# Seven stage boundaries of a two-block transformer kernel: token parts, affine and split in PSUM, half norms on ScalarE

## What is computed

```python
# first block, i = 0, 1 (mix is the sconv/SSD mixer, then the forgetting attention)
x = layer_norm(ALPHA * x + mix, ln_mix_g[i], ln_mix_b[i])
x = layer_norm(ALPHA * x + conv_ffn(x, ...), ln_ffn_g[i], ln_ffn_b[i])
# second block, i = 0, 1 (y is grouped-query attention, then the chunked gMLP)
h = modulate(rmsnorm(x, norm1_g[i]), sh1, sc1)
...
x = x + g1[:, None, :] * y
h = modulate(rmsnorm(x, norm2_g[i]), sh2, sc2)
x = x + g2[:, None, :] * sq_relu_mlp(h, mlp_w_in[i], mlp_w_out[i])
```

## Time and profile before

| | us |
|---|---|
| median of three runs (2811.03 to 2811.69) | 2811.19 |
| the profiled execution | 2811.43 |
| its span in the trace | 2809.5 |
| PE busy | 2783.7 |
| DVE / POOL / ACT busy | 1303.3 / 1140.6 / 1081.2 |

### The profile page before, as it was taken

The page is one execution under the profiler, slowest core; times in us unless marked ns, Lnnn a source line. Parts: engine busy times, 40 slices in busy tenths (PEclk is TensorE's granted clock), DMA queues, the critical chain, the costliest instruction groups (busy, mean ns, idle before and its releaser), DMA issues.

```text
span 2809.5 us, 37915 instructions
## 1 busy us (share of the span) xinstructions
PE 2783.7 (99%) x13890; PEld 2287.7 (81%) x13890; DVE 1303.3 (46%) x1516; ACT 1081.2 (38%) x1574; POOL 1140.6 (41%) x472
## 2 busy tenths in 40 slices
PE   9999999999999999999989999999999999999999
PEld 8788888888878788888877788888888888888887
DVE  4157568863441658874276651123423642411232
ACT  3443443343332544333345643334333223432332
POOL 4333434444434024444435035444344434444443
PEclk9999999999999999999999999999999999999999
DMA  5322238742333027753321023332243322233332
GB/s 160 90 69 74 90 103 267 239 140 88 99 88 95 9 76 232 244 169 102 97 73 45 2 74 106 97 105 98 86 135 94 90 78 103 90 92 96 104 98 75
DMA packets 319812, 299.95 MB, mean 107 GB/s; under 512 B 16268, under 2 KB 251224, under 8 KB 319576
## 3 DMA queue, kind: packets, MB, share of 16 engines
q1 hardware_dynamic: 304680, 236.70, 28.2%
q10 hardware_dynamic: 15024, 61.75, 6.3%
HBM read 296.30 MB, written 2.11 MB: 106 GB/s over the span
## 4 chain that ended last, share of the span: by engine, by line
PE 46%; issue 36%; POOL 16%; DVE 1%; ACT 0%; POOLq 0%; DVEq 0%; ACTq 0%
POOL wlo L558 16%; PE ps L2034 8%; PE ps L2035 8%; PE ps L2036 8%; PE ps L1892 6%; PE ps L1894 6%; PE ps L1893 6%; PE ps L2319 1%; PE ps L2255 1%; PE ps L2284 1%; PE ps L2394 1%; PE ps L2065 0%; PE ps L2067 0%; PE ps L2066 0%; PE ps L1897 0%
## 5 line engine op out<-in xcount | busy, mean ns | idle before, releaser
L558 POOL TENSOR_TENSOR wlo<-raw,whi 128x1024 fp32r<-128x1024 f32 x444 | 1115.3, 2515 | 1630.6 <-ACT whi L616 1630.3
L1892 PE MATMUL ps<-xhi,whi 128*128 128x512 f32 x1824 | 718.0, 394 | 0.3
L1894 PE MATMUL ps<-xhi,wlo 128*128 128x512 f32 x1824 | 710.3, 389 | 0.0
L1893 PE MATMUL ps<-xlo,whi 128*128 128x512 f32 x1824 | 709.9, 389 | 0.0
L616 ACT ACTIVATE whi<-raw 128x1024 fp32r<-128x1024 f32 x444 | 466.3, 1052 | 288.9 <-PE ps L2036 167.8
L2034 PE MATMUL ps<-whi,ahi 128*128 128x512 f32 x1184 | 461.4, 390 | 0.7 <-DVE alo L1396 0.7
L2036 PE MATMUL ps<-whi,alo 128*128 128x512 f32 x1184 | 460.7, 389 | 0.0
L2035 PE MATMUL ps<-wlo,ahi 128*128 128x512 f32 x1184 | 460.6, 389 | 0.0
L1892 PEld LDWEIGHTS ps<-xhi,whi 128*128 128x128 f32 x1824 | 342.5, 188 | 73.1 <-issue 3.2
L1894 PEld LDWEIGHTS ps<-xhi,wlo 128*128 128x128 f32 x1824 | 342.3, 188 | 71.7
L1893 PEld LDWEIGHTS ps<-xlo,whi 128*128 128x128 f32 x1824 | 342.6, 188 | 71.0 <-issue 1.4
(11 more groups left out here) (282 smaller groups left out, 2858.0 us busy)
## 6 DMA issues: line engine op xcount, KB each, us to landing
adaraw<-in_ada_w ACTq DMA_DIRECT2D x64, 768.0 KB, 6.1
raw<-in_ffn_w_up SPq DMA_DIRECT2D x88, 512.0 KB, 4.0
raw<-in_mlp_w_in SPq DMA_DIRECT2D x64, 512.0 KB, 4.0
raw<-in_mlp_w_out SPq DMA_DIRECT2D x64, 512.0 KB, 3.7
raw<-in_gmlp_w_in SPq DMA_DIRECT2D x48, 512.0 KB, 3.8
raw<-in_sc_ssm_w_in SPq DMA_DIRECT2D x44, 512.0 KB, 3.8
raw<-in_ffn_w_down SPq DMA_DIRECT2D x44, 512.0 KB, 3.6
raw<-in_fox_w_in SPq DMA_DIRECT2D x24, 512.0 KB, 3.8
```

The costliest lines, as they stand in the source:

```text
L558: pool.tensor_tensor(wlo[:, j], raw[:, j], whi[:, j].bitcast(F32), ALU.subtract).then_inc(w_lo, 1)
L1892: pe.matmul(out, lh, rh, start=start, stop=False)
L1893: pe.matmul(out, lh, rl, start=False, stop=False)
L1894: return pe.matmul(out, ll, rh, start=False, stop=stop)
```

## The change

- `pe_busy` is no longer called at a boundary, and `xf` and `junk` are gone. The affine writes back to PSUM in place, and DVE splits out of PSUM.
- Blocks 0 to 3 go in token parts: at the six ordinary boundaries two parts of 256 tokens, at boundary 4 parts of 256, 128 and 128. Blocks 4 to 7 stay 512 wide.
- Part 1's eight transposes (tiles 0 and 1) stand inside the last tile of the tail, part 2's eight inside unit 2's products for part 1. `pe_f` runs blocks 0 to 3 of units 0 to 2 in 72 products of 128x256 and blocks 4 to 7 in 36 of 128x512. qkv and gv take the token tiles of a part.
- ScalarE does six of the eight half norms, at 1 to 3 with scale rstd and bias minus mean by rstd, for which DVE has a new small instruction a tile (`neg_mean`).
- At 1 and 3 the residual's four scales stand in and behind DVE's splits of blocks 6 and 7, and its four shifts go into the first FFN iteration, two behind each `hid_ff`. At 2 all eight stand beside the fqk stage's own splits.
- At 4 the last four units of dn1 ("deep") run tile by tile, with their activations held in the upper half of the split buffers, 24 products to a tile.
- The DMAs of `wf_raw` and `wsraw` are issued behind all affines of their boundary. In `pe_gm` tiles 0 and 1 of units 0 and 1 go first, and the transposes of `wsraw` wait for all eight blocks.

```diff
+    def act_xt_part(act, q, scale, bias, h, cols=PART):
+        c = cols[h]
+        for k in range(4):
+            act.wait_ge(xt_tp, XT0[q] + 4 * h + k + 1)
+            act.activation(ps[:, k, c], ps[:, k, c], ACT.Identity, scale=scale(k), bias=bias(k)).then_inc(xt_ev, 1)
...
+    def dve_xt_part(dve, q, h, cols=PART, ks=range(4)):
+        c = cols[h]
+        for k in ks:
+            dve.wait_ge(xt_ev, EV0[q] + 4 * h + k + 1)
+            dve.tensor_copy(xhi[:, k, c], ps[:, k, c]).then_inc(xt_hi, 1)
+            dve.wait_ge(xt_hi, XT0[q] + 4 * h + k + 1)
+            dve.tensor_tensor(xlo[:, k, c], ps[:, k, c], xhi[:, k, c].bitcast(F32), ALU.subtract).then_inc(xt_lo, 1)
...
+        dve_ln_moments(dve, r, name, 0)
+        dve_ln_moments(dve, r, name, 1)
+        for t in range(2):
+            dve_ln_inverse(dve, r, t)
+            norm(t, 0)
+        dve_ln_moments(dve, r, name, 2)
...
+        dve_xt_part(dve, r + 1, 0, ks=(2,))
+        dve_ln_moments(dve, r, name, 3)
+        dve_xt_part(dve, r + 1, 0, ks=(3,))
...
+        scale(0)
+        dve_xt(dve, r + 1, ks=(6,))
+        scale(1)
+        dve_xt(dve, r + 1, ks=(7,))
+        scale(2)
+        scale(3)
...
+                    if lo == 0:
+                        shift = resid_steps(dve, 2 * L)[1]
+                        shift(2 * b)
+                        shift(2 * b + 1)
...
+            for h in range(2):
+                for k in range(4):
+                    pe.wait_ge(xt_lo, XT0[q] + 4 * h + k + 1)
+                    for e in range(2):
...
+                        product(e, k, PART[h])
+                if h:
+                    for k in range(4, KD):
+                        pe_xt_late(pe, q, k)
+                for k in range(4):
...
+                    if not h and k == 2:
+                        pe_xt_part(pe, q, 1)
+                    product(2, k, PART[h])
+            for k in range(4, KD):
+                pe.wait_ge(xt_lo, XT0[q] + 4 + k + 1)
...
+    def pe_t_deep(pe, name, q):
+        H, S, A = PAIRS[name], U0[name], A0[name]
+        for t in range(NT):
+            for m in range(2 * H - 4, 2 * H):
...
+                if t == NT - 1:
+                    ins.then_inc(unit_done, 1)
+                    if m == 2 * H - 3:
+                        pe_xt_part(pe, q, 0)
...
+        for i, tiles in enumerate(DOUBLE_TILES):
+            last = i == 2
+            pe.wait_ge(res_add, 24 + (6, 7, 8)[i])
+            units(0, [0], blocks=XT0[4] + 4 * i, tiles=tiles, done=last)
+            if last:
+                for k in range(4, KD):
+                    pe_xt_late(pe, 4, k)
+            units(0, [1], blocks=XT0[4] + 4 * i + 2, tiles=tiles, done=last,
+                  mid=None if last else lambda: pe_xt_part(pe, 4, i + 1))
...
             if j == 1:
-                pe.wait_ge(xt_ev, 48)
+                pe.wait_ge(xt_lo, XT0[7])
                 pe.wait_ge(ws_in, 16)
```

More of the change, by code:

```diff
@@ L82 @@
 GU_SLOTS = 4
-NRM_ORDER = ((0, 0), (1, 0), (0, 1), (2, 0), (3, 0), (1, 1), (2, 1), (3, 1))
-KEEP_BUSY = (0, 18, 0, 16)
+PARTED = (1, 2, 3, 5, 6, 7)
+XT0 = [0]
+for _q in range(8):
+    XT0.append(XT0[-1] + (12 if _q in PARTED else 16 if _q == 4 else 8))
+EV0 = [_n - 8 for _n in XT0]
+PART = (slice(0, 256), slice(256, 512))
+DOUBLE_TILES = ((0, 1), (2,), (3,))
+DOUBLE_PART = (slice(0, 256), slice(256, 384), slice(384, 512))
+DEEP = "dn1"
 KEEP_START = (14, 24)
-NRM_COUNT = {t: NRM_ORDER.index((t, 0)) + 1 for t in range(4)}
 SMALL_AFTER, FORGET_AFTER, CUM_AFTER = 3, 8, 11
@@ L618, in build_in, with a_parts @@
     AHEAD = 3
+    def a_parts(name, m):
+        first = 2 * PAIRS[name] - 3
+        if name == DEEP and first <= m < first + 2:
+            return ahi2[:, m - first], alo2[:, m - first]
+        return ahi[:, m % 2], alo[:, m % 2]
     def bank_f(j):
@@ L1407, in dve_jit @@
         after_h0()
-        run(dve, H - 2, lambda e, j: step(H + 2, 2, e, j))
+        if name != DEEP:
+            run(dve, H - 2, lambda e, j: step(H + 2, 2, e, j))
+        else:
+            run(dve, H - 5, lambda e, j: step(H + 2, 2, e, j))
+            for m in range(2 * H - 3, 2 * H):
+                hi, lo = a_parts(name, m)
+                dve.wait_ge(a_hi, A + m + 1)
+                dve.tensor_tensor(lo, src[:, 2 * (m - H):2 * (m - H) + 2], hi.bitcast(F32), ALU.subtract).then_inc(a_lo, 1)
     def wait_tile(eng, r, name, t):
@@ L1674, in dve_qkv @@
         dve.wait_ge(qkg_in, 48)
-        dve.wait_ge(xt_lo, 40)
+        dve.wait_ge(xt_lo, XT0[5])
         for z in range(2):
@@ L1963, in unit @@
             ins.then_inc(unit_done, 1)
-        for s, v in first:
-            pe.wait_ge(s, v)
         if q == 0:
@@ L2019, in pe_f, with pe_t_unit @@
                     unit(i * RING + j, j)
-    def pe_t_unit(pe, start, e, j, bank0, lh, ll, first, blocks=None):
+    def pe_t_unit(pe, start, e, j, bank0, lh, ll, first, blocks=None, tiles=range(NT), done=True, mid=None):
         slot = (start + j) % RING
@@ L2027, in pe_t_unit @@
         for k in range(2):
+            if mid and k:
+                mid()
             if blocks is not None:
                 pe.wait_ge(xt_lo, blocks + k + 1)
-            for t in range(NT):
+            for t in tiles:
                 out = ps[:, bank0 + t]
```

370 lines of the change are left out of this document (222 added, 148 removed).

## The result

The changed kernel takes 2796.43 us in the median of five runs (2794.49 to 2797.13), the kernel before 2811.19 (2810.92 to 2811.69, five runs too); the ratio is 0.9946, with a 95% interval of 0.9935 to 0.9956. The profiled execution took 2796.46, against 2811.43 before, so 14.97 us went. The forecast was 2791, with 2785 to 2803 as its range: it was faster as forecast, by three quarters of the 20 us that the sum promised. The narrower range of 2787 to 2795, which was given the chance of 0.58, was missed by 1.4 us.

The account below looks back on a forecast made before the run. PE's stream bounds the kernel, except in 54.15 us of gaps at seven boundaries, set by the latency of the DVE, PE, ACT, DVE chain. The terms summed to -20.3 from 2811.43, giving 2791 us, range 2785 to 2803.

Parts of the forecast that it names:

- The gap and the half products: Boundaries 1 and 3: the 5.87 us gap goes; 72 half products at 0.12 us replace 36 full ones, +0.45 us.
- rival A: Half products take 0.165 to 0.188 us each: +2 us at five boundaries, 2801 us, or 2806 at 0.188; chance 0.10.
- Boundaries 1 and 3: Gap -5.87, transposes +1.31, half products +0.45, waits +2.1: -2.0 us each.
- "some 0.5" for part 2: Boundaries 1 and 3: part 2's first block follows tile 3's norm through ACT and DVE, costing some 0.5 us more.
- The shifts: Four shifts in the first FFN iteration may take 9 us, mostly covered by slack: +0.5 us for boundaries 1 and 3 together.
- rival C: Shifts hold DVE, then ACT, so PE waits in the first FFN iteration at boundaries 1 and 3: 2795.5 us; chance 0.08.
- Boundaries 5 and 7: The same as boundaries 1 and 3, with the RMS norm's two instructions a tile but no moments: -2.1 us each.
- Boundary 2: As boundary 1, but a weight copy queues behind the wait for `wf_raw`: -1.7 us, ends -2.0 and 0.
- Boundary 4: Of 21.57 us beside the products 7.9 remain, with no fall of the clock: -13.7 us, ends -9 and -14.5.
- The 0.6 for a late `wlo`: Boundary 4, inside the deep tail: 0.6 us allowed for a late `wlo`, within the 7.9 us beside the products.
- Boundary 6: Late DMA of `wsraw` leaves PE idle 5 us, +0.5, and the clock falls, +2.3: +2.8 us, ends -0.9 and +4.
- rival E: Without dummies the clock falls at the five ordinary boundaries and at 6: 2825 us; chance 0.04.

Follow-up runs that it names:

- the run with the late DMA: The kernel before, with only the DMA of `wsraw` at boundary 6 issued behind the eight affines instead of ahead of them: 2815.95 us, ratio 1.0015.
- the third mend: Changed kernel with early DMA of `wsraw`, its transposes behind unit 2, and ScalarE's copy of gv's unit 2 behind part 1's affines: 2790.98 us, ratio 0.9925.
- the early DMA: Changed kernel with the DMA of `wsraw` issued right behind the last square, ahead of part 2's affines: 2793.08 us, ratio 0.9933.
- the first run of the mends together: Changed kernel with `wsraw` early, its transposes behind unit 2, scales behind block 7's split, and 16 dummy transposes in the attention: 2791.05 us, ratio 0.9924.
- the second step at boundary 6: Changed kernel with the DMA of `wsraw` early and PE's transposes of it one unit later, behind gv's unit 2: 2793.32 us, ratio 0.9935.

## Why the prediction was right, and where its sum was off

**The gap and the half products: right.** The 5.87 us became 0.23. A half product takes 0.12, the value taken between 0.109 and 0.188, so rival A did not happen, and the nearest row, with the same columns on half the rows, was the right one to go by. That the load's duration is no price holds: 188 ns on the record beside a pitch of 120. The rule on weight loads from the Trainium skill, "TensorE: Matmul & The Clock Gate", section "LDWEIGHTS (loading the stationary operand)", 107 ns for 128 columns, would have given 0.107; the measured 0.119 is above it, and the measurement decides.

**Boundaries 1 and 3: the step that failed.** The sum ended at block 3 and "some 0.5" for part 2, and charged the residual only for its shifts. The part "The shifts" named the four that moved into the FFN; they took 1.21 us each there and cost nothing. It passed over the scales that stand between the splits of blocks 6 and 7. A row for the price of such an instruction was there, 4.55 us for two shifts of the same size, and so was the order of instructions. One scale in front of block 7's split, stretched to 2.79 us by GpSimd, is 1.5 us at each: moving them gave them back, and boundary 2, which has none there, shows it without an edit. The rule of the Trainium skill that rival C named ("SBUF — State Buffer", "Who interferes with whom") fits: this scale has two SBUF inputs and took 2.79, while the split of block 6 at 409.24, with one SBUF input and beside the same GpSimd instruction, took 0.69. The prediction had the right rule and laid it on the wrong four instructions.

**Boundaries 5 and 7: a term too small.** They gained 1.4, not 2.1. That forecast leaves 2.06 us for waits (5.92 - 1.31 - 0.45 - 2.1); PE's rows at 5 show idle times of 0.36 for the norms of part 1, 1.48 for block 3 and 0.25, and each restart costs 0.16 more than its idle time says, because a product's end is modelled: at boundary 1 the starts at 395.15 and 396.67 are 1.52 apart, 1.40 over the pitch, where the row says 1.24. Three such waits are 0.5 us of the 0.7 that is missing. This is read from the rows, no run tried it. At 1 to 3 the same term was not too small: by starts the wait is 1.40 for block 3 and 0.34 for part 2's first block, where 1.6 and 0.5 were taken.

**Boundary 2: too cautious.** `wf_raw` landed in 2.3 us rather than the 4 to 6.8 that bounded it, with nothing left ahead of it. No loss, and at -2.3 the boundary came out beyond the -2.0 that was given as its better end, by the two waits above.

**Boundary 4: right in mechanism, 0.8 us or more short.** Forecast -13.7, measured -12.9 against the one trace of the kernel before. In the run with the late DMA that kernel's boundary 4, untouched, was 0.6 us shorter, and against that the gain is 12.3: the miss is 0.8 to 1.4. The run without the deep tail shows that the pace of 5.46 us a tile is what keeps PE fed. The 0.6 for a late `wlo` in the deep tail was the right size on the wrong operand: the wait of 0.95 us (1.1 by starts) is for `alo`, a subtraction with two SBUF inputs that took 2.75 us beside GpSimd instead of 1.23. The parts wait 0.61, 1.29 and 0.24, 2.6 us by starts, less than the 3.1 taken.

**Boundary 6: right, but by luck in its second half.** +2.8 forecast, +2.9 measured, and 1.75 to 3.2 in other profiles of the same edit. The wait was 3.98 rather than 5. One reason is that ScalarE issued the DMA at 2014.76 us, while its last two affines ended at 2016.14: the forecast counted from the affine's end. The clock took the rest. The move of the DMA alone in the old kernel costs 5.9. What the prediction did not see is that two more waits stood right behind it. And whether the clock falls there was a draw too: behind 2.2 us of waiting it fell in two profiles and not in a third.

**The attention: not in the sum.** 0 forecast, +1.5 measured. The step that failed is a reading: one row with a clock of 1.00 behind 1.94 us of idle time was taken as what such a stretch does. It is one draw; in eight of the ten other profiles without dummies there it cost 0.7 to 1.5 us. The prediction used the row as its reason against rival E as well. That rival still did not happen: PE's idle stretches at the boundaries are 1.2 to 1.5 us between products at full pace, and no fall is in the trace there. The run without dummies shows that its mechanism is real, and the chance of 0.04 that it got rested on a row that does not carry it.

## What to carry to other kernels

When a wait on the critical path is shortened, list every instruction between the two that matter on the engine that is waited for, not only those that the change moves, and price each beside what the other engines do then. A wait that ends last hides those behind it: at one boundary a DMA, a split and a weight copy stood within 2 us, and the whole gain came only with the third mend (+2.9, +0.5, -0.1, -1.8). Dummy work on TensorE wasn't waste here: it filled idle stretches with little work around them, and taking it out alone cost 14.6 us. The change could drop it because the token parts put real products in its place. One trace is one draw of the granted clock; before a row of it is used as a rule, look at a second execution.

## What the runs showed of the hardware

- An idle stretch of 1.94 us in the attention, the same in each kernel, was followed by a granted clock of 1.00 in three traces and by 1.2 GHz in eight, for a loss of 0 to 1.5 us. Sixteen transposes of an identity in it gave 1.00 in all three profiles that had them.
- Idle stretches of 1.2 to 1.5 us with products at full pace on both sides never brought the clock down, in eight places of the changed kernel's trace. One of 2.2 us between such products was followed by a fall in two profiles (the early DMA; the first run of the mends together) and by none in a third (the second step at boundary 6). In the gaps without dummies, with idle stretches of 1.8 to 2.2 and 1.5 to 1.8 us and 12 transposes around them, it fell at all six ordinary boundaries, for 1.9 to 2.9 us each.
- With two SBUF inputs a VectorE instruction of 128x1024 took 2.6 to 2.8 us beside a GpSimd instruction on SBUF, and 1.22 without it. A 128x512 subtraction with one input in PSUM took 0.69 beside one, as without.
- A 128x256 split out of PSUM in two instructions takes 0.80 us (at boundary 1 those of blocks 0 and 1 start at 391.57 and 392.36), as estimated from the one of 512.
